# Five SwiGLU stages with Strassen products: one product, four load transfers and ScalarE's copies of a pair in another order

## The reference

```python
def swiglu_ffn_2(x, w_gate, w_up, w_down):
    return (jax.nn.silu(x @ w_gate) * (x @ w_up)) @ w_down
```

## Time and profile before

| what | us |
|---|---|
| three runs | 2744.68, 2744.72, 2724.52 |
| median | 2744.68 |
| profiled execution, its time | 2743.0 |
| its span, first to last instruction | 2741.1 |
| TensorE busy in the span | 2691.6 |
| VectorE busy in the span | 1829.4 |
| ScalarE busy in the span | 1294.7 |

### The profile page before, as it was taken

One profiled execution on the slowest core, in us unless ns is written; L12 is line 12 of the kernel. 1 busy time (PEld: TensorE's weight loads), 2 busy tenths in 40 slices (PEclk: granted clock), 3 DMA queues, 4 the chain that ended last, 5 costly groups with the idle time before them and its releaser, 6 DMA issues.

```text
span 2741.1 us, 53376 instructions
## 1 busy us (share of the span) xinstructions
PE 2691.6 (98%) x22432; PEld 2566.5 (94%) x22432; DVE 1829.4 (67%) x2650; ACT 1294.7 (47%) x2052; POOL 239.4 (9%) x212
## 2 busy tenths in 40 slices
PE   8999999999999999999999999999999999999998
PEld 8976998999999999997899999999999987999998
DVE  6776753788626888348869884338886367598843
ACT  4465524555524555246754553225554246455531
POOL 0010201000000000018810000000000000100000
PEclk9999999999999999999999999999999999999999
DMA  6320331223332233321113333342333342123332
GB/s 211 107 76 18 117 115 47 85 86 108 116 101 78 93 105 114 101 91 55 47 55 93 105 106 111 97 150 90 108 109 116 93 134 90 55 88 108 109 110 74
DMA packets 76267, 265.10 MB, mean 97 GB/s; under 512 B 8389, under 2 KB 10565, under 8 KB 75777
## 3 DMA queue, kind: packets, MB, share of 16 engines
q1 hardware_dynamic: 69408, 248.93, 29.4%
q10 hardware_dynamic: 5632, 8.39, 0.8%
q0 software_dynamic: 992, 4.42, 0.5%
HBM read 253.29 MB, written 8.42 MB: 95 GB/s over the span
## 4 chain that ended last, share of the span: by engine, by line
PE 87%; DVE 5%; ACT 3%; DMA 2%; issue 2%; POOL 1%; DVEq 0%; SPq 0%; POOLq 0%; ACTq 0%
PE bank L650 47%; PE bank L816 28%; PE bank L705 2%; DMA w_raw<-in_w_gu 2%; DVE bank L3015 1%; PE bank L770 1%; DVE w_lo L2272 1%; POOL c_acc L3288 1%; PE bank L1467 1%; PE bank L1546 1%; ACT w_hi L1625 1%; PE bank L1385 1%; PE bank L994 1%; PE bank L1566 1%; PE bank L1121 1%
## 5 line engine op out<-in xcount | busy, mean ns | idle before, releaser
L2272 DVE TENSOR_TENSOR w_lo<-w_raw,w_hi 128x1024 fp32r<-128x1024 f32 (+1 forms) x296 | 358.0, 1213 | 351.2 <-ACT w_hi L1625 184.5
L816 PE MATMUL bank<-t_hl,w_hi 128*128 128x256 f32 x2752 | 526.4, 280 | 10.1 <-issue 7.6
L816 PEld LDWEIGHTS bank<-t_hl,w_hi 128*128 128x128 f32 x2752 | 439.7, 188 | 14.8 <-issue 14.2
L1625 ACT ACTIVATE w_hi<-w_raw 128x1024 fp32r<-128x1024 f32 (+1 forms) x296 | 298.0, 1023 | 237.3 <-PE bank L650 157.5
L650 PE MATMUL bank<-h_hi,w_hi 128*128 128x256 f32 x1936 | 389.0, 282 | 12.5 <-DVE w_lo L2272 12.0
L650 PE MATMUL bank<-t_hl,w_hi 128*128 128x256 f32 x2128 | 387.2, 281 | 0.0
L650 PE MATMUL bank<-h_hi,w_lo 128*128 128x256 f32 x1936 | 379.9, 278 | 0.0
L650 PE MATMUL bank<-h_lo,w_hi 128*128 128x256 f32 x1936 | 379.9, 278 | 0.0
L816 PE MATMUL bank<-t_hl,wx 128*128 128x256 f32 x1720 | 353.4, 278 | 0.0
L650 PE MATMUL bank<-t_hl,w_lo 128*128 128x256 f32 x1672 | 333.2, 281 | 0.0
L816 PE MATMUL bank<-t_hl,w_lo 128*128 128x256 f32 x1720 | 324.8, 278 | 0.0
(11 more groups left out here) (394 smaller groups left out, 4611.1 us busy)
## 6 DMA issues: line engine op xcount, KB each, us to landing
w_raw<-in_w_gu SPq DMA_DIRECT2D x220, 512.0 KB, 3.6
w_raw<-in_w_dn SPq DMA_DIRECT2D x80, 512.0 KB, 3.6
w_raw<-in_w_dn SPq DMA_DIRECT2D x40, 384.0 KB, 3.2
w_raw<-in_w_pw SPq DMA_DIRECT2D x24, 512.0 KB, 3.6
w_raw<-in_w_in SPq DMA_DIRECT2D x22, 512.0 KB, 4.6
w_raw<-in_w_xkv SPq DMA_DIRECT2D x16, 512.0 KB, 3.5
w_raw<-in_w_kv SPq DMA_DIRECT2D x16, 512.0 KB, 3.5
stick_qkv<-t ACTq DMA_DIRECT2D x24, 256.0 KB, 2.0
```

What stands on the lines that cost most here:

```text
L816: last = nc.tensor.matmul(pair_bank(s, which), w[:, i * P:(i + 1) * P], o, start=start and i == 0 and m == 0, stop=stop and i == 3 and m = ...
L1625: nc.scalar.activation(w_hi[:, at:at + n], w_raw[:, at:at + n], ACT.Copy).then_inc(w_hi_made, 1)
L2272: V.tensor_tensor(w_lo[:, at:at + n], w_raw[:, at:at + n], w_hi[:, at:at + n].bitcast(f32), sub).then_inc(w_lo_made, 1)
```

## The change

TensorE: `last_product` moves from behind S1 to behind A12, so a pair is A11, S1, S2, A12, A22 of the pair before, S3, S4. SyncE: from the third pair of a stage on, each pair is loaded with four transfers of 256 KB, in the order A22, A11, A12, A21; each waits for the last reader of its own block (A22 for `low_a22`, the others for the products A11, A12 and S3 of the pair two before). ScalarE: the copy for S3 and A22 stands behind the copy for S1 and S2, and `seed` Z now stands between `high_a` and `high_s12`. VectorE: the sum S4 and `low_a` move ahead of `inner`. The counts in the waits follow (`SPLIT0` counts the extra transfers of the stages before). The order within the last pair of a stage is not edited.

```diff
                         gate, up = block(u), block(u + 1)
+                        sp.wait_ge(w_lo_made, U0[name] + u - 2)
+                        sp.dma_start(block_of(w_raw, s, 3), up[:, BLOCK:2 * BLOCK]).then_inc(raw_in[2 * s + 1], 16)
+                        sp.wait_ge(pair_used, 6 * (g - 2) + 1)
+                        sp.dma_start(block_of(w_raw, s, 0), gate[:, 0:BLOCK]).then_inc(raw_in[2 * s], 16)
                         sp.wait_ge(pair_used, 6 * (g - 2) + 4)
-                        sp.dma_start(w_raw[:, 2 * s * UNIT:(2 * s + 1) * UNIT], gate).then_inc(raw_in[2 * s], 16)
+                        sp.dma_start(block_of(w_raw, s, 1), gate[:, BLOCK:2 * BLOCK]).then_inc(raw_in[2 * s], 16)
                         sp.wait_ge(pair_used, 6 * (g - 2) + 5)
-                        sp.dma_start(w_raw[:, (2 * s + 1) * UNIT:(2 * s + 2) * UNIT], up).then_inc(raw_in[2 * s + 1], 16)
+                        sp.dma_start(block_of(w_raw, s, 2), up[:, 0:BLOCK]).then_inc(raw_in[2 * s + 1], 16)
...
                         product(s, "S1", "T1", "W", True, True).then_inc(pair_used, 1)
-                        if not first:
-                            last_product(name, f, p - 1, 1 - s)
                         pe.wait_ge(seeded, 3 * g + 1)
...
                         product(s, "A12", "B21", "X", False, True).then_inc(pair_used, 1)
+                        if not first:
+                            last_product(name, f, p - 1, 1 - s)
...
                         high_a(0, 0, 0)
+                        high_s12(0, 0)
                         high_s3(0, 0)
-                        high_s12(0, 0)
                         high_s4(0, 0)
...
                             high_a(p + 1, 1 - s, it + s)
-                            high_s3(p + 1, 1 - s)
                         seed(p, s, "Z", "Y", 3)
                         if at_end:
                             a_part(3, 4, 5)
                             split(down, 0, 12, 1)
                         else:
                             high_s12(p + 1, 1 - s)
+                            high_s3(p + 1, 1 - s)
                             high_s4(p + 1, 1 - s)
...
                 def low_s12(p, s):
-                    dve.wait_ge(pair_hi, 3 * (PAIR0[name] + p) + 3)
+                    dve.wait_ge(pair_hi, 3 * (PAIR0[name] + p) + 2)
...
                         dve.wait_ge(w_used, U0[name] + n0 + 2 * p - 2)
+                    dve.wait_ge(pair_hi, 3 * (PAIR0[name] + p) + 3)
...
                         low_s4(p, s)
-                        sums(p + 1, 1 - s, it + s, "S3", "S2")
+                        sums(p + 1, 1 - s, it + s, "S3", "S2", "S4")
+                        low_a(p + 1, 1 - s)
                         inner(p - 1, 1 - s)
-                        sums(p + 1, 1 - s, it + s, "S4")
-                        low_a(p + 1, 1 - s)
                         low_s12(p + 1, 1 - s)
```

More of the change, by code:

```diff
@@ L159 @@
 NPAIRS = dict(PAIRS)
+SPLIT0, _ = starts([(n, NPAIRS[n] // 2 - 1 if n in NPAIRS else 0) for n, _, _ in STAGES])
 NORM, _ = starts([(n, stats) for n, _, _, stats in NORMS])
@@ L1620, in split @@
                     return
-                act.wait_ge(raw_in[slot], 16 * (q + 1))
+                act.wait_ge(raw_in[slot], 16 * (q + 1 + SPLIT0[name]))
                 if not (isinstance(q, int) and q == 0):
@@ L1665, in high_a @@
                     u = U0[name] + n0 + 2 * p
-                    act.wait_ge(raw_in[2 * s], 16 * ((U0[name] + n0) // RING + turn + 1))
+                    act.wait_ge(raw_in[2 * s], 16 * ((U0[name] + n0) // RING + SPLIT0[name] + 2 * turn + 1))
                     if p == 0:
@@ L2365, in sums @@
                             for slot in (2 * s, 2 * s + 1):
-                                dve.wait_ge(raw_in[slot], 16 * ((U0[name] + n0) // RING + turn + 1))
+                                dve.wait_ge(raw_in[slot], 16 * ((U0[name] + n0) // RING + SPLIT0[name] + 2 * turn + 1))
                             if p == 0:
```

## The result

| | before | after |
|---|---|---|
| runs | 22 | 22 |
| median, us | 2741.32 | 2721.96 |
| lowest to highest | 2724.29 to 2750.37 | 2714.64 to 2727.87 |
| profiled execution, span | 2743.0, 2741.1 | 2726.45, 2724.7 |

The ratio is 0.9934, with a 95% interval of 0.9922 to 0.9947: the change makes the kernel 19 us, 0.7%, faster. Forecast were 2710, a range of 2696 to 2752, and a move of more than 1% with a chance of 0.45 against 0.51 for less.

A forecast was written before the change was run, and what follows sets the result against it. TensorE, busy 98% of the span, was taken as the bound, with gaps and two matmul paces; gaps -4.4, pairs' pace -10.0 and down stages -19.1 sum to -33.5 from 2743.0, so 2710 us, range 2696 to 2752.

The forecast's parts named there:

- The gaps: TensorE's waits in the pairs: start and steady ones go, three short ones per stage come; net -4.4 us.
- the 13.3: Gaps expected after the change: five stages of 0.1 and 0.94 us in pair 1, 1.63 in the last pair.
- The 17.7 of before: Gaps in the pairs before: 17.7 us, the rest of 33.7 us excess after 16.0 for slow matmuls.
- Loads: Pair transfers: A21 lands in 2.3 us, before VectorE asks for it; effect between 0 and 0.
- The pace: Matmuls start 113.3 or 117.8 ns apart, changing only at gaps; pairs gain 10.0 us, down stages 19.1.
- By 13 of 14 fast [...] I take four of five fast: Of 14 gaps of 0.4 us or more entered fast, 13 ended fast; so four of five stages taken as fast.
- the prediction's own sign: Wrong if gapless pairs change pace, long gaps end slow as often as fast, or fast-entered down stages slow by themselves.
- all fast: Rival: all pairs and down stages run at the fast pace; -44.3 us, 2699; its chance lies within 0.48.
- the forecast case: Pairs and down stages mostly or all at the fast pace; 2698 to 2722 us, chance 0.48.
- only the pairs become fast: Rival: down stages stay slow because of their own operands; 2729 us; chance 0.17, few fast down stages included.
- The rival on the slower side: The 0.94 us gap at S2 of pair 1 sets the slow pace every time; 2752.5 us, chance 0.15.
- The Trainium skill's single pace: Skill's 109 ns estimate for matmul starts, one pace; backs the rival that only gaps are gained, 2738.6 us, chance 0.20.

The follow-up runs named there:

- e6_big_loads: The changed kernel with the two 512 KB transfers of the kernel before in place of the four of 256 KB; median 2723.41 us.
- e1_end: The changed kernel, but in each stage's last pair ScalarE copies `seed` Z before the first down unit's split; median 2719.45 us.
- e10_end_gap: e8_no_gap with the change's own order of the last pair put back, A22 behind A12 in all pairs; median 2713.72 us.
- e9_pe_order: The kernel before with only TensorE's part of the change, A22 of the pair before behind A12; 2869.35 us in one run.
- e8_no_gap: The changed kernel, with A22 behind S1 in the last pair, and VectorE's last conv product and `t_low` of T4 put later at stage start; 2686.51 us.
- e3_both: e1_end with VectorE's `t_low` of T4 also moved behind `top` of pair 0; median 2730.18 us.

## Why the prediction was right or wrong

**The gaps: right.** The five waits at S3 of pair 0 and all gaps in steady pairs went. At A11 of pair 1 stand 0.14 us beyond a step (said 0.1), at S2 0.67 (0.94), at S3 of the last pair 1.73 (1.63). Together 12.7 us where 13.3 were said. S2 was nearer than I had it because `seed` Y starts 0.49 after `gated`, before its end, and A11 was itself 0.14 late. One term was left out of the 13.3: the step behind each gap is 0.19 to 0.22 us too, 1.6 us in all. The 17.7 of before, a remainder, held such steps. Like with like the gaps fell from 17.9 to 14.3, by 3.7 us (said 4.4).

**Loads: right in the result, off in a size.** A transfer of 256 KB lands in 2.8 us, not 2.3; VectorE still never waits for one in a pair, and e6_big_loads shows that even with the old ones nothing is lost. The section of the Trainium skill that the prediction took 2.6 us from (DMA: Bandwidth & Descriptors, "Anatomy of one DMA") gives its sum for transfers on the GpSimd path; these are on SyncE's queue, and the traces have 2.8 us for 256 KB and 3.6 us for 512 KB, where the sum gives estimates of 2.6 and 3.2.

**The pace: mechanism right, share wrong.** "By 13 of 14 fast [...] I take four of five fast" is the step that failed. In the profile after, two of five stages of pairs are slow and three of five down stages. The pairs' slow matmuls went from about 3550 to 2780, -3.4 us where -10.0 were said; the down stages gained 9.1 (two of five) where 19.1 were said. With the gaps that is -16.2, and the span fell by 16.4. By the prediction's own sign it was wrong here: of the ten long gaps of the changed kernel (0.71 or 0.78 us at S2, 1.85 us at S3) five ended fast and five slow, "as often as".

The range held, but it reaches from "all fast" to "slower than before" and so says little, and the measured 2721.96 is at the upper edge of the forecast case (2698 to 2722). That the time came this near 2710 owes something to the draw: the traces of the changed kernel, e6_big_loads and e1_end have three, four and five of five stages of pairs fast, behind start gaps of the same places and nearly the same lengths.

Why the share was wrong: I read the 14 earlier gaps as draws whose odds depend on their length, and took over the odds of the long ones. Five of the 14 were the same gap, 1.79 us at S3 of pair 0. Length is no such guide. The end gap, 1.85 us, entered fast turned slow in all twelve stages of three traces (after, e6_big_loads and e10_end_gap; three, four and five), and entered slow it turned fast in the other three; about 0.71 us at S2 of pair 1, entered slow, turned fast in all eight; 0.78 us there, entered fast, stayed so in eight of twelve. And e9_pe_order has 80 gaps of 1.85 us, 75 in other pairs and five in last pairs: of 36 entered fast 25 turned slow, of 44 entered slow 25 turned fast. Its five last pairs have the same gap at the same place as the changed kernel, and there only two of five turned. So within some kernels a gap at one place ends one way in stage after stage, but place and length together do not fix it either; over all it is near an even draw, somewhat more likely to turn the pace than to keep it. In the changed kernel's trace the new end gap turned exactly those down stages slow whose pairs had been fast. Other runs probably differ: the median of the 22 is 4.5 us below the profiled one, about what one down stage is worth (an estimate: 1081 matmuls times 4.45 ns, 4.8 us), and no trace shows them. The rival "only the pairs become fast" came nearer in size (2729), but its reason was not the one at work: not the down stages' operands, which run at 113.3 ns in e8_no_gap, but the gap ahead of them.

**The rival on the slower side** (the gap at S2 sets slow every time) did not come about in this kernel, but its mechanism is real: e3_both is 8 us slower than the changed kernel with four of five stages slow.

**The Trainium skill's single pace.** The section that the prediction cites (the Trainium skill, TensorE: Matmul & The Clock Gate, "Wait — 56ns, not 53.3ns?") has one start-to-start time at the upper clock, for matmuls back to back. Here each matmul has its own weight load, and all ten traces have two times, at a granted clock of 1.00 in the windows read (the earlier trace rows and the two above); the difference is worth up to 54 us of this kernel's pairs and down stages (29.9 + 23.9, an estimate from the counts).

**What stays open:** what the two paces are, and what sets which of them a gap ends in. Its length, its place and the pace ahead of it are not all of it (0.25 us at A11 of pair 1, entered fast, ended fast in 17 and slow in 13 of 30 stages of the six traces that have it).

## What to carry to other kernels

On an engine that is 98% busy, divide time by count in stretches without waits before costing a change: two paces of the same instruction 4% apart were worth more here than all waits together. A copy that frees the bottleneck engine belongs ahead of every copy for the next round; look at the first and the last round by themselves, since an order that is right in the steady rounds can be wrong there. A small wait can cost more than its length, and taking out all but one can make things worse, so close them all. A small scatter between runs (here 2.2 us against 12.9 and 19.7, four runs each) may be a sign that they are closed.

## What the runs showed of the hardware that was not expected

- TensorE's f32 matmuls of 128x128 by 256 columns start 113.3 or 117.8 ns apart at the same granted clock, over hundreds of microseconds, and the pace changed only at gaps (0.14 us and more from start to start) in the pairs and down stages of the ten traces. There, at the slow pace, one weight load in three is shown as 192 ns long and the others as 187 or 188; at the fast pace none is over 188.
- The 1.85 us gap at S3 of the last pair turned the pace round in 15 of 15 stages, from either side, in three profiled executions (after, e6_big_loads, e10_end_gap), but in two of five in e9_pe_order, where gaps of the same length in other pairs did so in 48 of 75.
- Moving one ScalarE instruction of 0.37 us ahead of one of 1.06 us made the kernel 38 us faster (2741.81 to 2703.81); removing all gaps of the pairs made it 54 us faster (2740.49 to 2686.51), of which the gaps themselves are some 18. The rest is the pace: in the two traces slow matmuls cost the pairs 15.8 us and the down stages 23.1 before, and nothing after.
